# Attention on one core: the fourth score piece of a block moves behind a values piece and a transpose

## What is computed

```python
def one(qblk):                      # 128 queries of every head
    s = jnp.einsum('bqhd,bkhd->bhqk', qblk, k, preferred_element_type=jnp.float32) * scale
    p = jax.nn.softmax(s, axis=-1).astype(v.dtype)
    return jnp.einsum('bhqk,bkhd->bqhd', p, v)
```

## Time and profile before

| | |
|---|---|
| runs | 2356.21, 2358.72, 2360.28 us; median 2358.72 |
| profiled execution | 2355.62 us, its span 2353.8 us |
| TensorE busy | 96% of the span |
| attention's score and values pieces | from 754.3 to about 1380 us |
| a block of a middle group (n = 9), b = 0 to 3 | 9.50, 9.60, 10.14, 9.12 us |

### The profile page before, as it was taken

One profiled execution on the slowest core, in us unless ns is written; L12 is line 12 of the kernel. 1 busy time (PEld: TensorE's weight loads), 2 busy tenths in 40 slices (PEclk: granted clock), 3 DMA queues, 4 the chain that ended last, 5 costly groups with the idle time before them and its releaser, 6 DMA issues. The chain is left out here.

```text
span 2353.8 us, 34599 instructions
## 1 busy us (share of the span) xinstructions
PE 2256.6 (96%) x11426; PEld 1894.3 (80%) x11426; DVE 1404.0 (60%) x2146; ACT 1156.8 (49%) x2160; POOL 1025.7 (44%) x762
## 2 busy tenths in 40 slices
PE   5999998999998999999999989998999999999998
PEld 4888887989897778777777768887888888877886
DVE  7333336444445777767677751215999999983342
ACT  4555534222324655555555545556556565653432
POOL 6322222222223432323333132332989999982454
PEclk9999999999999999999999999999999999999999
DMA  7533323434343533434342224331111211253653
GB/s 298 179 134 134 134 76 139 152 127 151 127 145 118 150 105 98 107 94 116 85 119 82 90 104 143 118 123 42 44 59 41 68 54 43 74 177 114 174 161 107
DMA packets 196117, 271.15 MB, mean 115 GB/s; under 512 B 10532, under 2 KB 137764, under 8 KB 191398
## 3 DMA queue, kind: packets, MB, share of 16 engines
q1 hardware_dynamic: 191398, 261.43, 34.7%
q10 hardware_dynamic: 4608, 8.39, 1.0%
HBM read 183.27 MB, written 86.51 MB: 115 GB/s over the span
## 5 line engine op out<-in xcount | busy, mean ns | idle before, releaser
L2353 POOL TENSOR_TENSOR conv_g<-conv_g,product 128x1024 f32<-128x1024 f32 x160 | 384.9, 2408 | 34.3 <-ACT product L2402 24.6
L2500 DVE SCALAR_TENSOR_TENSOR ps_b<-u,cols,ps_b 128x1024 f32<-128x1024 f32 x304 | 391.7, 1288 | 9.2
L2616 PE MATMUL ps_a<-ho_hi,wp_lo 128*128 128x512 f32 x768 | 300.8, 392 | 6.8 <-DVE h_left L2556 6.8
L2617 PE MATMUL ps_a<-h_left,wp_hi 128*128 128x512 f32 x768 | 300.0, 391 | 0.0
L2618 PE MATMUL ps_a<-ho_hi,wp_hi 128*128 128x512 f32 x768 | 299.9, 391 | 0.0
L2402 ACT ACTIVATE product<-u,cols 128x1024 f32<-128x1024 f32 x160 | 183.3, 1151 | 170.0 <-POOL conv_g L2353 168.7
L1605 ACT ACTIVATE pt_hi<-ps_pt 128x512 fp32r<-128x512 f32 x256 | 154.4, 604 | 197.5 <-PE ps_pt L1801 197.3
L1716 DVE TENSOR_TENSOR pt_lo<-ps_pt,pt_hi 128x512 fp32r<-128x512 f32 x256 | 175.9, 688 | 119.7 <-ACT pt_hi L1605 116.9
L1660 POOL TENSOR_TENSOR v_lo<-v_st,v_hi 128x512 fp32r<-128x512 f32 x64 | 84.2, 1316 | 237.0 <-DVE v_hi L1692 237.0
L1706 DVE TENSOR_REDUCE mx<-ps_s 128x1 f32<-128x512 f32 x248 | 167.0, 684 | 21.3 <-PE ps_s L1793 20.3
L2616 PEld LDWEIGHTS ps_a<-ho_hi,wp_lo 128*128 128x128 f32 x768 | 145.0, 189 | 38.6 <-DVE h_left L2556 8.7
(11 more groups left out here) (449 smaller groups left out, 5629.0 us busy)
## 6 DMA issues: line engine op xcount, KB each, us to landing
scratch_ret_pack<-pack SPq DMA_DIRECT2D x14, 1280.0 KB, 5.4
pack<-scratch_ret_pack SPq DMA_DIRECT2D x14, 1280.0 KB, 7.0
k_st<-scratch_k_t SPq DMA_DIRECT2D x64, 256.0 KB, 3.5
v_st<-scratch_v SPq DMA_DIRECT2D x64, 256.0 KB, 3.7
ada<-in_ada_w_dram SPq DMA_DIRECT2D x16, 768.0 KB, 6.2
wp_raw<-in_od_w_in_dram SPq DMA_DIRECT2D x24, 512.0 KB, 4.1
xt<-in_x_dram SPq DMA_DIRECT2D x16, 512.0 KB, 6.1
ada<-in_ada_w_dram SPq DMA_DIRECT2D x8, 1024.0 KB, 8.8
```

What stands on the lines that cost most here:

```text
L2353: pool.tensor_tensor(half(conv_g, h), half(conv_g, h), product[adds(c, i, h) % 2][:], ALU.add).then_inc(added, 1)
L2500: dve.scalar_tensor_tensor(acc[h], units(c, k, h), params(c, k), acc[h], ALU.mult, ALU.add).then_inc(tap, 1)
L2616: pe.matmul(dst, lo[:, k, :], h_hi[:, k, t], start=k == 0, stop=False)
L2617: pe.matmul(dst, hi[:, k, :], h_lo[:, k, t], start=False, stop=False)
```

## The change

Only the order in which TensorE's stream is written changes, in every block that has both scores and turns. Before, the order is S0 T0 S1 T1 S2 **S3 V-2 V-1 T2 V0 T3 V1**. After, it is S0 T0 S1 T1 S2 **V-2 T2 S3 V-1 T3 V0 V1**. The other four engines' streams are the same, word for word.

```diff
                         scores(n, s, b, 2)
+                        values_next(-2)
+                        turn_next(2)
                         scores(n, s, b, 3)
-                        values_next(-2)
                         values_next(-1)
-                        turn_next(2)
+                        turn_next(3)
                         values_next(0)
-                        turn_next(3)
                         values_next(1)
```

## The result

| | runs | median us | against before, same chip |
|---|---|---|---|
| before | 4 | 2357.82 | |
| changed | 4 | 2369.55 | ratio 1.0044, 95% interval 1.003 to 1.0057 |
| changed, measured again twice | 9 and 10 | 2367.5, 2368.15 (before beside them 2360.19) | 1.0032 (1.0021 to 1.0043), 1.0036 (1.0025 to 1.0046) |

The forecast was 2362.0 with a range up to 2367.0. The kernel is slower by 0.3 to 0.4%, where 0.14% was forecast. (The first pair rests on four runs each; its interval overlaps those of the repeated ones.) Attention, from its first score piece to its last transpose, took 625.1 us in the profile of before and 637.1 in that of the changed kernel: 12.0 of the 15.1 us by which the two spans differ. The other 3 lie behind attention, where the two kernels are the same; the granted clock was at its lower level, 0.50, for 33 us there instead of 22.

A forecast was written before the change was run, and what follows sets the result against it. Attention was taken as bound nearly everywhere by TensorE's own work. Ten loop groups at +0.37 (+3.7) and written-out groups at -0.45 gave +3.25 us on the profiled 2355.62; with the median 3.1 higher, forecast 2362.0, range 2355.5 to 2367.

The forecast's parts named there:

- the sum: Whole kernel: +0.37 us per loop group, +3.7 for ten, -0.45 for the written-out groups, +3.25 together.
- Term A: From b = 0 to b = 1: T3 ends earlier, so S0 of b = 1 waits less; gain of 0.35 us per loop group.
- Term B: From b = 1 to b = 2: later V-1 delays `o_t` and VectorE's train, so T1 of b = 2 comes 0.44 us later.
- the last rival: VectorE's `q_hi` cast ahead of T1 of b = 2 falls from 1.50 to about 0.5, giving about 2349 us; chance 0.05.
- Terms C and D: S0 of b = 3 and of the next b = 0: each 0.03 late plus 0.11 for the weight load, 0.14 us.
- the upper bound of the forecast: Bias to exponential ahead of S0: 0.33 us at most, making S0 0.12 late and the kernel +5.95.
- the cover: TensorE's pieces between S3 and the next S0: 2.50 us instead of 3.64, against a chain of 2.53 in the loop.
- TensorE's own work: All attention blocks: work does not change, S3 +0.10 and V1 -0.10; every block without a wait stays at 9.12 us.
- the second (the score chain becomes the bound): Bias to exponential in the loop takes 0.33 or more, each 0.1 us costing 3 us over three S0 a group; chance 0.24.

The follow-up runs named there:

- the swap: `ada` load issued behind the `v_st` load, still in b = 0: old order 0.9993 (2358.36 us), new order 1.002 (2364.05 us), both against the kernel before.

## Why the prediction was wrong

**The step that failed** is a wait that the sum put at nothing. The prediction saw it in groups 6, 8, 10 and 12 ("T1 of b = 0 waits too, where VectorE passes the head of the loop"), and then took ten loop groups at +0.37 with no term for it. Nothing asked what VectorE did in that wait, or whether the change could lengthen it; "DMA issues and SP's queue do not move" is where the question was closed, but VectorE's branch moved against them. The runs show the head gap at 3.20 us on average before and 4.09 after: +3.6 us over four heads, about half of the 7.3 to 8.0 by which the changed kernel's repeated medians lie above before. With the +5.0 that the rest of attention gave (below), the kernel would by these numbers have stayed within the range without it. That the transfers at the branch lengthen the gap was shown by moving the load away, and that their place matters by the swap. Why the new order puts them where they lengthen it more often was shown only in part: the branch comes 3.7 us behind the issue of `ada` instead of 3.3 to 3.6.

**Term A** was right: S0 of b = 1 starts 6.41 after T1 of b = 0 in the loop's odd groups, where 6.40 was forecast, and alone it makes the kernel faster. **Term B** was right: 13.71 to 13.77 from S0 of b = 1 to T1 of b = 2, where 13.75 was forecast. The whole train on ScalarE and VectorE moved, as these rows of group 9 show, which answer to the earlier trace rows:

```profile
1104.62 0.60 ACT L1636 ACTIVATE o_t<-ps_ot 128x512 f32<-128x512 f32 x1 [3.47 <-PE ps_ot L1812]
...
1106.11 0.69 ACT L1598 ACTIVATE probs<-ps_s,bias 128x512 f32<-128x512 f32 x1
```

```profile
1107.73 1.51 DVE L1699 CAST q_hi<-q_st 128x512 fp32r<-128x512 f32 x1
1109.28 0.69 DVE L1701 TENSOR_TENSOR q_rot<-qr_st,q_rot 64x512 fp32r<-64x512 f32 x1
1109.99 0.69 DVE L1716 TENSOR_TENSOR pt_lo<-ps_pt,pt_hi 128x512 fp32r<-128x512 f32 x1
```

From `o_t` to the exponential there are 1.49, as before, and from `q_hi` to `pt_lo` 2.26, as before. `q_hi` still takes 1.51, so the last rival did not come. T1's idle time was 0.78, not the 1.1 of the forecast, because S0 of b = 2 was late as well (at 1106.94, 0.83 behind its exponential) and took up that part. The prediction had this 0.34 and did not take it off the idle time.

**Terms C and D** were a little mis-sized. Alone they came to 0.11 and 0.24 in odd groups, 0.35 together where 0.28 was forecast. S0 of b = 3 is hardly late (2.53 after S3's end, 2.52 where nothing waits), with a first matmul of 0.44, and S0 of b = 0 is the one that is really late. ScalarE's exponential at the end of b = 3:

```profile
1125.68 0.69 ACT L1598 ACTIVATE probs<-ps_s,bias 128x512 f32<-128x512 f32 x1 [2.14 <-DVE bias L1712]
```

It starts 0.32 behind the bias at 1125.36, next to the upper bound of the forecast. The prediction had one value, 0.24, for all three S0; the loop has two and nothing between. It is 0.32 to 0.33 at the end of b = 3 in odd groups (5 to 11) and of b = 0 in even ones, and 0.19 at the end of b = 2, of b = 3 in even groups and of b = 0 in odd ones. Why is open. The 0.19 stood in the loop before the change too, behind the bias of group 8 at 1077.98, though the prediction found no such row:

```profile
1078.17 0.69 ACT L1598 ACTIVATE probs<-ps_s,bias 128x512 f32<-128x512 f32 x1
```

The S0 behind the late exponential:

```profile
1125.73 0.40 PE L1810 MATMUL ps_ot<-pt_hi,v_lo 128*128 128x512 f32 x1
...
1126.51 0.50 PE L1789 MATMUL ps_s<-k_hi,q_lo 128*128 128x512 f32 x1
1126.85 0.39 PE L1790 MATMUL ps_s<-k_lo,q_hi 128*128 128x512 f32 x1
```

V1 takes 0.78 instead of 0.69 to the next start, so S0 is 0.09 late, and its first matmul holds the next one off for 0.34 where 0.23 is the rule: the 0.11 for the load, as taken from the earlier trace rows. The Trainium skill says that TensorE pulls weight loads ahead of matmuls in flight ("TensorE: Matmul & The Clock Gate", in "Part 2: What happens when you issue a matmul"). For an S0 whose wait is only just met the trace does not show that: load and matmul both start at 1126.51, and the 0.11 is paid. Behind even groups b = 3 grew by 0.30 and not by 0.18, since the bias starts 0.57 behind the maximum over the four banks and not 0.31:

```profile
1086.17 0.16 DVE L1710 TENSOR_REDUCE m<-mx 128x1 f32<-128x4 f32 x1
1086.74 0.15 DVE L1712 TENSOR_SCALAR bias<-m 128x1 f32<-128x1 f32 x1 [0.42 <-DVE m L1710]
```

This was there before as well and hidden under the cover (1077.40 to 1077.98 in group 8):

```profile
1077.40 0.16 DVE L1710 TENSOR_REDUCE m<-mx 128x1 f32<-128x4 f32 x1
1077.98 0.15 DVE L1712 TENSOR_SCALAR bias<-m 128x1 f32<-128x1 f32 x1 [0.41 <-DVE m L1710]
```

**TensorE's own work** is not quite unchanged. A block without any wait took 9.17 instead of 9.12: the pieces add up that much longer in the new order, 0.01 here and there. Over 60 blocks that is 3 us at most; where T1 of b = 2 waits anyway, part of it does not count.

**The rest of the sum.** With `ada` moved, all of attention came to +5.0, where +3.25 was forecast. The ten loop groups gave about +4.4 instead of +3.7: +0.4 each in the odd ones and +0.5 on average in the even ones, which the prediction took to be like group 9. The written-out groups gave about +0.5 instead of -0.45. The forecast for groups 2, 3 and 14 has a slip besides the pieces: it counts the 0.11 of the load once in the gain of 0.49 and again in the loss of 0.33, and without that it is -0.05 each, not -0.16. They measured +0.1 to +0.2. With the heads' +3.6 all this is 8.6. The two repeated pairs of profiles differ in attention by 7.4 and 8.7, their medians by 7.3 and 8.0.

Of the rivals, the second (the score chain becomes the bound) is right in its mechanism where the exponential starts 0.32 behind the bias, at one or two S0 of a loop group and not at three. That its 2364.5 to 2368 comes near the repeated medians is luck: the head gap, which brings them there, stands in no rival.

## What to carry to other kernels

A wait that the profile puts down to an engine which had long been done is a question to answer before the change is costed, above all at the head of a hardware loop. Here the code itself seems to come by the queues of the loads, and issuing the big load elsewhere brought the new order from 0.32 to 0.36% over before to 0.18%. An order pays only in the blocks whose wait it shortens: in b = 0 the next S0 waited for T3, and the new order in that block alone was 0.2% faster than before, with the loop written out 0.5% (0.9949; writing out alone gives 0.26%). The same order in all four blocks of the loop was 0.3 to 0.4% slower. Before adding up costs per group, measure an even and an odd one, and ask which part of the written-out code lacks a step that the loop has (here `hold` and the branch): the same order cost 0.4 to 0.6 us in a loop group and 0.1 in a written-out one.

## What the runs showed of the hardware

- From VectorE's branch back to the head of the hardware loop to its next instruction 2.8 us passed at the least and 4.6 at the most, at the 60 heads of 15 profiles; ScalarE, TensorE's sequencer, GpSimd and SP passed theirs in 0.16 to 0.31 in the profiles of before and the changed kernel. Behind VectorE's last branch, where the loop ends, the next `pt_lo` came after 0.69 and 0.99 in these two.
- The excess over 2.8 comes with loads (768 and 256 KB) under way at the branch, though not at every head: gaps of 2.8 came with them too. With the larger one issued elsewhere twelve gaps of twelve were 2.8 to 3.1.
- Writing the loop out (ten groups more of code in each stream) cost nothing that shows: with the old order the kernel was 0.26% faster than before.
- An idle time of TensorE of 1.93 us was once followed by 3.4 us at the 1.2 GHz level, and idle times of 1.2 to 1.9 us at other heads were not. In group 1 TensorE was idle for 1.97 or 1.98 us in every profile, and 3.4 us at that level followed in 7 of 18.
